# Group norm behind the core of an RWKV-7 mixer: centred values, bonus and variance ahead of the gate products, logarithm and exponential in two groups of four tiles

## The reference

```python
_, y = lax.scan(rwkv7_step, S0, seq)            # the core
m = jnp.mean(y, axis=-1, keepdims=True)         # over the 64 channels of a head
var = jnp.mean(jnp.square(y - m), axis=-1, keepdims=True)
y = ((y - m) * lax.rsqrt(var + GN_EPS)).reshape(B, T, D) * ln_g + ln_b
bonus = (jnp.sum(rh * kh * r_k, axis=-1, keepdims=True) * vh).reshape(B, T, D)
out = ((y + bonus) * g).astype(h.dtype) @ w_o   # g = sigmoid(xg @ g1) @ g2
```

## Time and profile before

| | us |
|---|---|
| median of 3 runs | 2715.67 |
| lowest, highest | 2712.27, 2724.11 |
| the profiled execution, by the clock of the runs | 2721.26 |
| its span in the profile | 2719.5 |
| PE busy / DVE / ACT / POOL | 2560.2 (94%) / 1419.9 (52%) / 1175.8 (43%) / 994.5 (37%) |
| mean granted clock of TensorE | 0.976 |

### The profile page before, as it was taken

How to read it: one execution, slowest core, us unless ns; L and a number is a source line. 1 busy time by engine, 2 the same in 40 slices (tenths; PEclk the granted TensorE clock), 3 DMA queues, 4 the chain that set the end, 5 groups by cost and what they waited for, 6 DMA issues and landing times.

```text
span 2719.5 us, 62750 instructions
## 1 busy us (share of the span) xinstructions
PE 2560.2 (94%) x25306; PEld 2393.8 (88%) x25306; DVE 1419.9 (52%) x2004; ACT 1175.8 (43%) x1709; POOL 994.5 (37%) x488
## 2 busy tenths in 40 slices
PE   6998997989999999999999999999998989999997
PEld 6887884887999999877888999999997659999997
DVE  7565654212677753797726677632162335555522
ACT  7744444443444433324634344433437433444432
POOL 3333220451344444324322444544342103444452
PEclk8899998999999999999999999999999899999998
DMA  4221001241222233313211222333221102222231
GB/s 142 77 70 41 1 9 67 94 140 47 86 93 93 93 98 104 116 63 109 78 62 63 93 93 93 102 108 109 78 93 57 37 1 81 90 93 95 98 101 62
DMA packets 61088, 219.36 MB, mean 81 GB/s; under 512 B 6689, under 2 KB 7073, under 8 KB 60321
## 3 DMA queue, kind: packets, MB, share of 16 engines
q1 hardware_dynamic: 57248, 206.19, 23.0%
q10 hardware_dynamic: 3712, 11.32, 1.1%
HBM read 213.29 MB, written 4.19 MB: 80 GB/s over the span
## 4 chain that ended last, share of the span: by engine, by line
PE 77%; DVE 10%; issue 8%; ACT 4%; POOL 1%; DVEq 0%; DMA 0%; ACTq 0%; POOLq 0%
PE psum L555 65%; DVE psum L2451 5%; PE psum L697 3%; PE psum L705 2%; POOL wl L504 1%; PE psum L1030 1%; PE psum L987 1%; PE psum L1205 1%; PE psum L1204 1%; ACT wh L1295 1%; DVE psum L2070 0%; DVE tmp L2036 0%; DVE fox_max L2644 0%; PE psum L1227 0%; DVE fox_p L2669 0%
## 5 line engine op out<-in xcount | busy, mean ns | idle before, releaser
L504 POOL TENSOR_TENSOR wl<-raw,wh 128x1024 fp32r<-128x1024 f32 x388 | 948.3, 2452 | 1574.8 <-ACT wh L1295 1574.6
L555 PE MATMUL psum<-acth,wh 128*128 128x256 f32 x3792 | 768.9, 285 | 34.5 <-DVE actl L1993 14.6
L555 PE MATMUL psum<-acth,wl 128*128 128x256 f32 x3792 | 757.0, 281 | 0.0
L555 PE MATMUL psum<-actl,wh 128*128 128x256 f32 x3792 | 756.6, 281 | 0.0
L1295 ACT ACTIVATE wh<-raw 128x1024 fp32r<-128x1024 f32 x388 | 407.3, 1056 | 531.9 <-PE psum L555 531.0
L555 PEld LDWEIGHTS psum<-acth,wh 128*128 128x128 f32 x3792 | 584.9, 190 | 53.2 <-issue 33.6
L555 PEld LDWEIGHTS psum<-actl,wh 128*128 128x128 f32 x3792 | 585.0, 190 | 0.0
L555 PEld LDWEIGHTS psum<-acth,wl 128*128 128x128 f32 x3792 | 584.5, 190 | 0.0
L2381 DVE TENSOR_TENSOR cu<-psum,rstd 128x512 f32<-128x512 f32 x132 | 91.0, 689 | 239.1 <-PE psum L555 224.3
L555 PE MATMUL psum<-hidl,wh 128*128 128x256 f32 x1056 | 205.9, 276 | 0.0
L555 PE MATMUL psum<-hidh,wl 128*128 128x256 f32 x1056 | 205.8, 276 | 0.0
(11 more groups left out here) (419 smaller groups left out, 4117.2 us busy)
## 6 DMA issues: line engine op xcount, KB each, us to landing
raw<-in_weights SPq DMA_DIRECT2D x388, 512.0 KB, 3.3
xt<-in_x SPq DMA_DIRECT2D x4, 512.0 KB, 6.3
xt<-in_x ACTq DMA_DIRECT2D x1, 2048.0 KB, 9.0
out_x<-xt ACTq DMA_DIRECT2D x4, 512.0 KB, 3.0
mem<-in_mem ACTq DMA_DIRECT2D x1, 1024.0 KB, 11.5
memn<-memh ACTq DMA_DIRECT2D x1, 1024.0 KB, 3.9
memn<-meml ACTq DMA_DIRECT2D x1, 1024.0 KB, 6.8
memh<-memn ACTq DMA_DIRECT2D x1, 1024.0 KB, 5.3
```

The costliest lines, as they stand in the source:

```text
L504: pool.tensor_tensor(wl[:, s, :], raw[:, s, :], wh[:, s, :].bitcast(F32), ALU.subtract).then_inc(split_done, 1)
L555: ins = pe.matmul(out[:, n:n + HALF], w, m[:, n:n + HALF], start=first and n == 0, stop=last and n + HALF >= out.shape[1])
```

## The change

PE no longer begins with the gate products. It centres tiles 0 and 1, then for each tile spreads the bonus, sums the squares and centres tile k+2, and makes the gate products behind that. The centred tile is read from PSUM twice by ACT: once squared, once multiplied by ln_g and written to `seq["r"]`, so that DVE's copy is gone. The bonus is split into a high and a low part in fp32r (`bonus_h`, `bonus_l`), and spread by four fp32r matmuls of 256 columns. Logarithm and exponential run in two groups of four tiles, with squares between. DVE reads the gate product from PSUM in its third operation on a tile; `g_all` and its evacuation by ACT are gone, and the bank is freed by a `sem_inc` ahead of the low part. The DVE tail goes tile by tile. The load of c_post is issued one round copy earlier, ahead of the last `core_copies`, behind a wait for the last two results of DVE in the core; the splits of units o2 and o3 by `weight_high` come behind the last `acth`.

```diff
 # PE
-            for j in range(KT):                      # gate products g2 first
-                ...
-            pe.wait_ge(cpost_in, 16)
-            pe.wait_ge(evacuated, plan("g2", "tile") + 8 + UC)
-            for k in range(KT + 2):
-                ...                                  # 951 centre, 952 bonus, 959 variance
-            pe.wait_ge(post_ln, KT)
+            def centre(k):
+                half, q = divmod(k, 4)
+                if k >= 2:
+                    pe.wait_ge(post_y, k - 1)
+                pe.matmul(bank[4 + k % 2], c_post[:, 4, :], seq["r"][:, 8 * half:8 * half + 8, q, :], start=True,
+                          stop=True).then_inc(mean_pe, 1)
+            def variance(k):
+                pe.wait_ge(post_sq, k + 1)
+                if k >= 2:
+                    pe.wait_ge(post_ln, k - 1)
+                pe.matmul(bank[6 + k % 2], blk64, sq[:, k % 2, :], start=True, stop=True).then_inc(var_pe, 1)
+            def bonus_spread(k):
+                half, q = divmod(k, 4)
+                if k >= 4:
+                    pe.wait_ge(post_v, k - 3)
+                for n in range(0, T, HALF):
+                    pe.matmul(bank[k % 4][:, n:n + HALF], bselr[:, q, :], bonus_h[:, half, n:n + HALF], start=n == 0, stop=False)
+                for n in range(0, T, HALF):
+                    ins = pe.matmul(bank[k % 4][:, n:n + HALF], bselr[:, q, :], bonus_l[:, half, n:n + HALF], start=False, stop=n > 0)
+                ins.then_inc(bonus_pe, 1)
+            pe.wait_ge(cpost_in, 16)
+            centre(0)
+            centre(1)
+            pe.wait_ge(bonus_split, 3)
+            for k in range(KT):
+                bonus_spread(k)
+                variance(k)
+                if k + 2 < KT:
+                    centre(k + 2)
+            for k in range(KT):                      # gate products g2 behind
+                ...
+                free_bank(t)
+                if k < 4:
+                    pe.wait_ge(post_v, k + 5)
+                ...
 # ACT
-            core_copies(NCH - 1, 2, 0)
             for g in range(2):
                 act.wait_ge(core_v[g], DVE_AT["T64", NCH - 1])
+            act.dma_start(c_post[:, :, :], ...).then_inc(cpost_in, 16)
+            core_copies(NCH - 1, 2, 0)
+            ...
+            act.activation(bselr[:, :, :], c_post[0:8, 0:4, :], ACT.Identity).then_inc(bonus_split, 1)
+            act.activation(bonus_h[:, :, :], bonus[0:8, :, :], ACT.Identity).then_inc(bonus_split, 1)
             act.dma_start(xt[:, :, 1:T + 1], dram["x"]).then_inc(xagain_in, 16)
             act.dma_start(mem[:, :, :], dram["mem"]).then_inc(mem_in, 16)
+            def squared(k):
+                half, q = divmod(k, 4)
+                act.wait_ge(mean_pe, k + 1)
+                if k >= 2:
+                    act.wait_ge(var_pe, k - 1)
+                act.activation(sq[:, k % 2, :], bank[4 + k % 2], ACT.Square).then_inc(post_sq, 1)
+                act.activation(seq["r"][:, 8 * half:8 * half + 8, q, :], bank[4 + k % 2].rearrange("p (c t) -> p c t", t=CH),
+                               ACT.Identity, scale=pc("ln_g", k)).then_inc(post_y, 1)
+            for k in range(4):
+                squared(k)
+                if k:
+                    logarithm(k - 1)
+            logarithm(3)
+            for k in range(4, 6):
+                squared(k)
+                factor(2 * k - 8)
+                factor(2 * k - 7)
+            for k in range(6, 8):
+                squared(k)
+                logarithm(k - 2)
+            logarithm(6)
+            logarithm(7)
+            post_high(0)
+            post_high(1)
+            for k in range(4, 8):
+                factor(k)
+            for k in range(2, 8):
+                post_high(k)
+            for k in range(2):
+                weight_high(UNIT0["g2"] + k + SLOTS)
 # DVE
+            dve.wait_ge(bonus_split, 2)
+            dve.tensor_tensor(bonus_l[:, :, :], bonus[0:8, :, :], bonus_h[:, :, :].bitcast(F32), sub).then_inc(bonus_split, 1)
+            def bonus_value(k):
+                v_ = seq_tile("v", k // 4, k % 4)
+                dve.wait_ge(bonus_pe, k + 1)
+                dve.tensor_tensor(v_, chunks(bank[k % 4]), v_, mul).then_inc(post_v, 1)
+            def post_value(n):
+                y_, v_ = (seq_tile(m, n // 4, n % 4) for m in "rv")
+                dve.wait_ge(post_a, n + 1)
+                dve.wait_ge(post_y, n + 1)
+                chain.step(dve.tensor_tensor(y_, chunks(grs[:, n, :]), y_, mul))
+                dve.wait_ge(post_v, n + 1)
+                chain.wait()
+                chain.step(dve.tensor_tensor(v_, y_, v_, add))
+                ...                                  # waits for gate product n and for the low part n-2
+                chain.wait()
+                dve.scalar_tensor_tensor(out=chunks(tmp[:, (g0 + n) % 2, :]), in0=v_, scalar=pc("ln_b", n),
+                                         in1=chunks(bank_of(plan("g2", "tile") + n)), op0=add, op1=mul).then_inc(val_ready, 1)
+            def post_low(k):
+                dve.wait_ge(hi_ready, g0 + k + 1)
+                dve.sem_inc(evacuated, 1)
+                dve.tensor_tensor(actl[:, k, :], tmp[:, (g0 + k) % 2, :], acth[:, k, :].bitcast(F32), sub).then_inc(lo_ready, 1)
+            for k in range(KT):
+                bonus_value(k)
+            for k in range(KT):
+                post_value(k)
+                if k:
+                    post_low(k - 1)
+            post_low(KT - 1)
```

More of the change, by code:

```diff
@@ L314, in build_program @@
         c_post = at("c_post", [P, 5, P], F32, yx_at)
-        grs = at("grs", [P, KT, T], F32, zone)
         delta0 = at("delta0", [P, 2, T], F32, yx_at + 10240)
-        g_all = at("g_all", [P, KT, T], F32, zone + 16384)
+        grs = at("grs", [P, KT, T], F32, zone + 16384)
+        bselr = at("bselr", [8, 4, P], F32R, yx_at + 14336)
+        bonus_h, bonus_l = (at("bonus_" + n, [8, 2, T], F32R, zone + 8192 + 4096 * j) for j, n in enumerate("hl"))
         cursor[0] = zone
@@ L939, in _ @@
                 for b in range(2):
-                    mm_ = product(bank[t % 4][:, :], u % SLOTS, 2 * (j % 4) + b, gmidh[:, b, :], gmidl[:, b, :],
+                    mm_ = product(bank[t % 4][:, :], u % SLOTS, 2 * (k % 4) + b, gmidh[:, b, :], gmidl[:, b, :],
                                   b == 0, b == 1)
-                mm_.then_inc(units_used if j % 4 == 3 else tile_full, 1)
-            pe.wait_ge(cpost_in, 16)
-            pe.wait_ge(evacuated, plan("g2", "tile") + 8 + UC)
-            for k in range(KT + 2):
[L947 to L959, removed]
@@ L960, in _ @@
[L960 removed]
+                mm_.then_inc(units_used if k % 4 == 3 else tile_full, 1)
             dense("o", "post", acth, actl, units=4)
@@ L1600, in _ @@
             g0, v0 = plan("post", "split"), plan("post", "val")
-            def post_ln_(k):
-                act.wait_ge(var_pe, k + 1)
-                act.activation(grs[:, k, :], bank[2 + k % 4][:, :], ACT.Ln, bias=b_gn, scale=1.0 / CH).then_inc(post_ln, 1)
-            for k in range(KT):
+            def squared(k):
                 half, q = divmod(k, 4)
-                act.wait_ge(post_v, k + 1)
+                act.wait_ge(mean_pe, k + 1)
                 if k >= 2:
                     act.wait_ge(var_pe, k - 1)
-                act.activation(sq[:, k % 2, :].rearrange("p (c t) -> p c t", t=CH),
-                               seq["r"][:, 8 * half:8 * half + 8, q, :], ACT.Square).then_inc(post_sq, 1)
-                if k >= 2:
-                    post_ln_(k - 2)
@@ L1615, in _, with logarithm @@
-            post_ln_(KT - 2)
-            post_ln_(KT - 1)
-            for k in range(KT):
+                act.activation(sq[:, k % 2, :], bank[4 + k % 2], ACT.Square).then_inc(post_sq, 1)
+                act.activation(seq["r"][:, 8 * half:8 * half + 8, q, :], bank[4 + k % 2].rearrange("p (c t) -> p c t", t=CH),
+                               ACT.Identity, scale=pc("ln_g", k)).then_inc(post_y, 1)
+            def logarithm(k):
+                act.wait_ge(var_pe, k + 1)
+                act.activation(grs[:, k, :], bank[6 + k % 2], ACT.Ln, bias=b_gn, scale=1.0 / CH).then_inc(post_ln, 1)
```

56 lines of the change are left out of this document (17 added, 39 removed).

## The result

Beside runs of the kernel before on the same chip the changed kernel took 2700.84 us (median of 6, 2698.77 to 2707.02) against 2714.68 (6 runs, 2712.27 to 2724.11): a ratio of 0.9944, 95% interval 0.9928 to 0.9959. The forecast was 2700, with 2694 to 2711 around it. The profiled execution took 2698.77 (span 2697.0), 22.5 us less than the profiled one of before. Not all of that is the change. I measure the changed stretch by itself, on ACT: from the start of the last core copy to the start of the evacuation of o1, when o1 is through.

What follows compares the result with a forecast made beforehand. PE was taken as busy nearly throughout, bounding the loop, then waiting on DVE's pace; 1.7, some 7.7 and most of 11 us, against 0.3, 2 and 2.6, gave 15.6 gained: 2715.67 to 2700, range 2694 to 2711.

Steps and rivals of the forecast that it cites:

- The mechanism: Loop to o1: most of the 11 us of gate products, now beside DVE's tail, would be gained.
- Entry, 0.3 us: End of the core: the earlier c_post issue delays a core copy, costing 0.3 us, between 0 and 0.9.
- The start-up of 4.4 us: Before the loop: ACT, casting and issuing x and mem first, lets sum of squares 0 start at 418.1.
- The loop: PE's loop: 2.45 us a tile against 2.97 before; ACT sets the pace after sum 4.
- The two added loads ... lie fully on the path: Inside the loop on ACT: two more table loads cost their full 2.6 us.
- the grouping is even: ACT's two groups: the loads' 2.6 us loss counted even with DVE's earlier start, about 3 us.
- The drain: Table loads on ACT: about 1380 ns extra drain, sum 2.8 us worse, some 2703; chance 0.14 together with slower DVE waits.
- the fall at 434: Rival, ACT-paced loop end: clock falls while PE idles, gain about 4 to 6 us, 2711; chance 0.09.
- The fall at 417, the slower rival: Rival, wait for the bonus split: clock falls, o0 ends 5 us later than now, 2721; chance 0.07.
- DVE's waits, 0.05 each: DVE's tail: a waiting operation costs 0.05 us, so a tile takes 2.76 us.
- the rival with 0.24: DVE's tail: waits cost 0.24 us each, gain 12.9 us, 2703; chance 0.14 together with the table drain.
- The sum: Start of o1: 461.8 instead of 477.4, gain 15.6 us, giving 2700 from the median 2715.67.

Runs made afterwards that it cites:

- The order alone: Kernel before with only the gate products moved behind the loop, c_post issued earlier and evacuations and splits moved along: 2712.65 us, ratio 0.9972.
- second profile: Changed kernel run once more, unchanged: 2704.65 us, ratio 0.9935, stretch 59.5 us against 56.9 in its first profile.
- one group: Changed kernel with all eight logarithms, then all eight exponentials, two table loads instead of four: 2703.04 us, ratio 0.9928.
- filled order: Changed kernel with bonus 6 ahead of sum 5, bonus 7 and gate tile 0 ahead of sum 6, gate tile 1 ahead of sum 7: 2702.09 us.
- pairs: Changed kernel with DVE's tail doing each kind of operation on two tiles side by side, both low parts behind: 2703.3 us, ratio 0.9938.
- late c_post: Changed kernel with the issue of c_post back behind x and mem and the last core copy: 2717.41 us, ratio 0.9991.
- fp32 bonus: Changed kernel with the bonus spread by one fp32 product, its split left out on ACT and DVE: 2702.01 us, ratio 0.9945.
- early splits: Changed kernel with the splits of o2 and o3 behind high parts 3 and 5: 2704.24 us, ratio 0.9951.
- the filled ones: Changed kernel with PE's gaps filled, 2702.09 us; also with DVE pairs and high parts 0, 1 ahead of logarithms 6, 7, 2693.66 us.

## Why the prediction was right, point by point

**The mechanism.** Right: the time comes from the gate products, which move beside DVE's tail. The order alone gave 9.1 us, and the gain of the whole change hangs on one early load: with c_post late the stretch was 72.2 us, longer than before. What the other edits add can't be summed from these runs, since the order alone carried a stall of 4.2 us of its own and ran o0 at the low clock.

**Entry, 0.3 us.** Too much: from DVE's last result to the last copy it was 5.25 us after and 5.50 before. So the early issue cost nothing that shows. The start-up of 4.4 us was 4.0. The forecast had ACT's first square set it, behind the issues of x and mem; these (409.13, 409.81) ran beside the activations of 409.08 and 409.62, and the first square was through at 411.13, well ahead of need. What set sum 0 was the path of the bonus: bonus_l ended 3.3 us behind the last copy (410.69 + 1.21) instead of 3.6, and the spreading took 0.67.

**The loop.** The bonus came at 0.67 instead of 0.46 "with a little for the switch", a tile at 2.58 instead of 2.45; four tiles of that are 0.5 us, and the earlier start paid for it. Sums 4 to 7 came within 0.2 us of the forecast (in the second profile sum 7 was 1.2 late, by the clock), with both waits where ACT's order had put them. The low cost of the fp32r bonus is shown: as one fp32 product a tile takes 2.96.

**"The two added loads ... lie fully on the path".** It fits in size but is not shown by itself: in one group sum 7 starts 2.9 us earlier, and that run takes out of the loop the four exponentials (1.15 and 1.14 us) as well as the two loads. That the grouping is even: right for this order of PE (stretches 56.7 and 56.9), no longer so with its gaps filled. Then the grouped kernel has its last low part through at 46.0 against 48.5 in one group, 2.5 us earlier. One group with gate tiles moved forward was not run; DVE waited there 3.03 us for ACT, not for PE. ScalarE: Activation LUTs, a page of the Trainium skill, says under "Table sets: the hidden batching unit" to finish all calls of one set first. The same section of the Trainium skill counts logarithm and exponential to one set, so that by it these loads would not be needed at all; the rows have a load at each of the four changes between the two (412.78, 423.28, 428.90, 440.63), and the rows decide. The loads last 1.28 us each, and the filled order shows that this is paid back where it lets another engine start on the first half. The drain that the same page of the Trainium skill gives is in no run here: 428.90 + 1.28 = 430.18, and the logarithm starts at 430.20; ahead of the load, too, nothing is lost (the copy before it ends at 428.88).

**The clock.** This step failed in part. The forecast had the fall at 434 as a rival worth 0.09, because "the longest here is shorter than the 7.7 us after which it fell". It did fall, behind a wait of 2.13 us. In all six profiles with a wait of 1.7 to 2.1 us before sum 6 (the changed kernel twice, pairs, late c_post, fp32 bonus, early splits) it fell during that wait or within 2 us behind it, and in the loops without such a wait (before, order alone, one group, the filled ones) it held. But the price was not the rival's 10 us: the low clock lasted 3.5 or 6.8 us, not until the end of o0, so that PE took back its lead over DVE. In the first profile it cost 1.6 us in the first gate tile (2.99 against 1.37), and the first value was 1.9 late; in the second profile 3.3. The fall at 417, the slower rival, did not come: the wait before the first bonus was 0.75 us, and the clock 1.00.

**DVE's waits, 0.05 each.** Too low. An operation that waits for the one ahead started 0.10 and 0.14 behind its end (440.47 + 0.69 to 441.26, 441.26 + 0.69 to 442.09), so a tile is 2.88 and not 2.76; over seven tiles 0.8 us., the nearest in kind, are of 256 columns; the rival with 0.24 was further off. In pairs, where none waits for its neighbour, the tail runs at 2.62.

**The sum.** From the last copy to o1: forecast 48.1, measured 51.0. The 2.9 us are 1.9 of the clock at the first value, 0.8 of the waits and 0.2 of the last parts. Against before, the gain at the start of o1 is 64.0 - 51.0 = 13.0, with 0.6 more by the evacuation because o1 no longer begins at the low clock, a term that the forecast had named and left out. At the start of o1 it is therefore 13.0 against the forecast's 15.6, at the evacuation 13.6. In the second profile the stretch gives 70.5 - 59.5 = 11.0, and the medians of the two calls give 13.8 and 18.1; the stretch of before is from one profile only, so the size is known no better than 11 to 18 us. That the median of 2700 was met to 0.8 us is luck in part: the gain was 1.8 us short of the forecast, and the median of before, from which it was set, was 1.0 lower in this call (2714.68 against 2715.67; in the other calls it was 2718 to 2723).

**Weights, nothing.** Right: PE never waited for the splits at 458.94. The forecast saw only that POOL was idle and that nothing was late; it did not see that idleness as a gain. With POOL at work beside the tail, DVE lost 1.3 us for each split. The sign of it stood in the forecast's own: that operation lasted 2.60 us, from 1064.73 to 1067.33, and POOL was splitting a weight beside it to 1067.05 (timeline of POOL, the kernel before):

```profile
1064.66 2.39 POOL L504 TENSOR_TENSOR wl<-raw,wh 128x1024 fp32r<-128x1024 f32 x1 [2.21 <-ACT wh L1295]
```

**Open.** Why the clock stayed low for 3.5 us in one execution of the changed kernel and 6.8 in another, with rows that agree up to the fall, no run settles.

## What to carry to other kernels

Put an engine's long block of independent work beside another engine's tail, and look first for the one load that the reversed order makes urgent: here the whole gain was lost when it came late. In the tight loop that remains, fill the short waits of PE with products that are ready anyway; a wait of 2 us cost 2 to 3 more through the clock behind it, and an order without such waits also repeats better. Splitting a batch to let a consumer start early gave nothing here by itself (56.9 against 56.7 us); with the gaps that it makes in PE's loop filled, the last low part came 2.5 us earlier than in one group.

## What the runs showed of the hardware

- A GpSimd tensor_tensor on SBUF held up a VectorE tensor_tensor with both operands in SBUF for as long as it ran: 2.00 and 1.99 us instead of 0.68, each ending 0.55 behind the end of the split. The operation with a PSUM operand beside it took its usual 0.75. The operation of the earlier trace rows, with one tensor operand in SBUF, lasted 2.60 us and ended 0.28 behind POOL's. The Trainium skill, SBUF — State Buffer, section "SBUF: two separate sides", says that the two engines share a pair of ports as an exclusive lock, and that the loser blocks for the other's whole instruction; the trace agrees with that, in that the loss is the whole of the time that was left of the split and no slower rate.
- DMA issues on ACT's queue (0.65 and 0.67 us) ran beside activations of the same engine (409.08 and 409.62) and cost them nothing.
- On VectorE an operation of 128x512 that needs the result of the one ahead starts 0.10 to 0.14 us behind its end; with another operation between, it starts before the one ahead has ended in the record (0.60 apart at 0.68 each).
- The granted clock of TensorE fell from 1.00 to 0.50 behind a wait of 2.13 us in an otherwise dense loop, while stretches with PE busy 5.49 of 8 us and then 1.70 of 4 were run at 1.00 in the same execution.
